# Gated DeltaNet layer on one core: GpSimd's order, two divided convolutions, and GpSimd's tile operations in quarters

## The reference

```python
h = rms_norm(x, norm_w) * (1 + scale) + shift            # scale, shift, gate from silu(c) @ ada_w + ada_b
q, k, v, z, b, a = split(h @ w_in)                       # 6160 columns
q, k, v = silu(causal_short_conv(concat(q, k, v), conv_w))   # 4 taps
q, k = l2_norm(q) * DK**-0.5, l2_norm(k)
beta, g = sigmoid(b), -exp(a_log) * softplus(a + dt_bias)
# S_t = exp(g_t)(I - beta_t k_t k_t^T) S_{t-1} + beta_t k_t v_t^T ; o_t = S_t^T q_t, chunk by chunk
o = gated_delta_rule_chunked(q, k, v, beta, g)
o = rms_norm(o, gdn_norm_w) * silu(z)
x = x + gate * (o @ w_out)
out = rms_norm(x, final_norm_w)
```

## Time and profile before

| | us |
|---|---|
| median of 3 runs | 1336.01 (1328.7 to 1340.26) |
| the profiled execution | 1332.38 |
| its span, first to last instruction | 1330.6 |
| PE busy | 1140.6 (86%) |
| DVE busy | 875.3 (66%) |
| POOL busy | 510.6 (38%) |
| mean granted TensorE clock | 0.945 of full speed |

### The profile page before, as it was taken

How to read it: one execution, slowest core, us unless ns; L and a number is a source line. 1 busy time by engine, 2 the same in 40 slices (tenths; PEclk the granted TensorE clock), 3 DMA queues, 4 the chain that set the end, 5 groups by cost and what they waited for, 6 DMA issues and landing times.

```text
span 1330.6 us, 18988 instructions
## 1 busy us (share of the span) xinstructions
PE 1140.6 (86%) x5572; PEld 926.7 (70%) x5572; DVE 875.3 (66%) x1881; ACT 444.0 (33%) x1022; POOL 510.6 (38%) x433
## 2 busy tenths in 40 slices
PE   1385589998899899998899989998899889999885
PEld 1353567877687778877787768777787778777763
DVE  4574657576776758575775758575766757586845
ACT  2232142333333242333333243323333243324333
POOL 2021253336433353345433353345433363345413
PEclk9588798999999999999999999999999999999998
DMA  6523132211322132211222122212212131212202
GB/s 240 206 73 111 37 88 51 58 36 48 74 50 56 48 77 51 56 36 49 73 50 56 52 72 51 56 39 65 62 47 52 52 81 42 56 39 70 51 33 110
DMA packets 143494, 88.34 MB, mean 66 GB/s; under 512 B 29350, under 2 KB 137032, under 8 KB 142408
## 3 DMA queue, kind: packets, MB, share of 16 engines
q1 hardware_dynamic: 143432, 87.73, 23.8%
HBM read 78.28 MB, written 9.44 MB: 66 GB/s over the span
## 4 chain that ended last, share of the span: by engine, by line
PE 52%; issue 19%; DVE 12%; POOL 8%; DMA 5%; ACT 3%; DVEq 0%; SPq 0%; POOLq 0%; ACTq 0%
PE bank L381 22%; PE bank L479 15%; DVE work L857 4%; POOL w_lo L1232 4%; POOL wo_lo L1238 2%; DMA w_raw<-in_gdn_w_in 2%; PE bank L522 2%; PE bank L439 2%; DVE y L890 2%; DMA work<-in_ada_w 2%; PE bank L532 1%; PE bank L535 1%; ACT w_hi L626 1%; PE bank L510 1%; PE bank L514 1%
## 5 line engine op out<-in xcount | busy, mean ns | idle before, releaser
L1232 POOL TENSOR_TENSOR w_lo<-w_raw,w_hi 128x1024 fp32r<-128x1024 f32 x96 | 244.7, 2549 | 425.3 <-ACT w_hi L626 425.3
L381 PE MATMUL bank<-h_hi,w_hi 128*128 128x512 f32 x768 | 323.7, 421 | 8.9 <-POOL w_lo L1232 4.5
L381 PE MATMUL bank<-h_hi,w_lo 128*128 128x512 f32 x768 | 319.1, 415 | 0.0
L381 PE MATMUL bank<-h_lo,w_hi 128*128 128x512 f32 x768 | 316.1, 412 | 0.0
L857 DVE SCALAR_TENSOR_TENSOR work<-pre,cw,work 128x512 f32<-128x512 f32 x192 | 212.1, 1104 | 23.6 <-DVE work L854 6.5
L381 PEld LDWEIGHTS bank<-h_hi,w_hi 128*128 128x128 f32 x768 | 150.2, 196 | 41.5 <-POOL w_lo L1232 8.0
L381 PEld LDWEIGHTS bank<-h_hi,w_lo 128*128 128x128 f32 x768 | 149.1, 194 | 31.4
L381 PEld LDWEIGHTS bank<-h_lo,w_hi 128*128 128x128 f32 x768 | 148.0, 193 | 29.0
L479 PE MATMUL bank<-wo_hi,og_hi 128*128 128x512 f32 x256 | 118.7, 464 | 53.4 <-POOL og_lo L1278 25.2
L652 ACT ACTIVATE work<-work 128x512 f32<-128x512 f32 x64 | 40.3, 629 | 302.3 <-DVE pre L865 176.8
L1278 POOL TENSOR_TENSOR og_lo<-work,og_hi 128x256 fp32r<-128x256 f32 x64 | 53.6, 837 | 208.8 <-ACT og_hi L686 208.8
(11 more groups left out here) (167 smaller groups left out, 1802.1 us busy)
## 6 DMA issues: line engine op xcount, KB each, us to landing
w_raw<-in_gdn_w_in SPq DMA_DIRECT2D x96, 512.0 KB, 4.0
work<-in_ada_w SPq DMA_DIRECT2D x8, 1024.0 KB, 5.0
w_raw<-in_gdn_w_out SPq DMA_DIRECT2D x16, 512.0 KB, 3.4
y<-in_x SPq DMA_DIRECT2D x2, 2048.0 KB, 9.1
work<-in_ada_w SPq DMA_DIRECT2D x8, 512.0 KB, 4.0
n_dram<-work SPq DMA_DIRECT2D x16, 256.0 KB, 3.4
out<-y SPq DMA_DIRECT2D x8, 512.0 KB, 2.6
t_dram<-work SPq DMA_DIRECT2D x16, 64.0 KB, 1.6
```

The source lines that it names most:

```text
L381: mm = nc.tensor.matmul(bank[m % 2][:, :], w[:, m % 2, k, :], h[:, k, half, :], start=(r == 0), stop=(r == MM - 1))
L1232: nc.gpsimd.tensor_tensor(w_lo[:, k % 2, :, :], w_raw_k[:, k % 2, :, :], w_hi[:, k % 2, :, :].bitcast(F32), ALU.subtract).then_inc(S["w_lo ...
```

## The change

Four edits:

- POOL in the recurrence of every unit but the last: tile 4 of `w_lo` stays in step 0; in step 1 the low half of the gated output now comes ahead of tile 5 of `w_lo`.
- DVE: the convolution `conv(u - 1, other, hd, 3)` at the head of the merge stage is divided: taps 0 and 1, then `merge_d_out(u, 0)`, then taps 2 and 3. The SiLU behind it (L874) moves behind `merge_p_out(u, 1)`. The convolution of q is divided too: taps 0 and 1 stay in step 1, taps 2 and 3 stand in step 2 behind `gate_o`.
- ACT, step 2: `og_high` now stands ahead of the tanh that waits for that convolution.
- POOL: `split_lo`, `split_wo` and `gate_wo` are four instructions on 128x256 each in place of one on 128x1024; only the last of the four raises the semaphore.

```diff
@@ ACT, recurrence
                     scale_x(u, par, c)
+                    if c > 0:
+                        og_high(u, c - 1)
                     if not last and c == 2:
                         tanh(u, 3, 1, cvq[:, other, :])
-                    if c > 0:
-                        og_high(u, c - 1)
@@ DVE, merge stage
                 silu(u - 1, 4, cvv[:, 0, :])
-                conv(u - 1, other, hd, 3)
+                conv(u - 1, other, hd, 3, range(0, 2))
                 merge_d_out(u, 0)
+                conv(u - 1, other, hd, 3, range(2, 4))
+                merge_p_out(u, 1)
                 silu(u - 1, 5, cvv[:, 1, :])
-                merge_p_out(u, 1)
                 if not last:
                     conv(u, par, nxt, 0)
@@ DVE, recurrence
                     if c > 0:
                         gate_o(u, c - 1)
+                    if not last and c == 2:
+                        conv(u, par, nxt, 1, range(2, 4))
                     passed(dve, "kv_done", u, c + 1)
...
                         elif c == 1:
-                            conv(u, par, nxt, 1)
+                            conv(u, par, nxt, 1, range(0, 2))
@@ POOL
             def split_lo(u, k):
                 passed(pool, "w_hi_done", u, k + 1)
                 passed(pool, "projected", u, k - 1)
-                nc.gpsimd.tensor_tensor(w_lo[:, k % 2, :, :], w_raw_k[:, k % 2, :, :],
-                                        w_hi[:, k % 2, :, :].bitcast(F32), ALU.subtract
-                                        ).then_inc(S["w_lo_done"], 1)
+                for j in range(0, KT, 2):
+                    i = nc.gpsimd.tensor_tensor(w_lo[:, k % 2, j:j + 2, :], w_raw_k[:, k % 2, j:j + 2, :],
+                                                w_hi[:, k % 2, j:j + 2, :].bitcast(F32), ALU.subtract)
+                i.then_inc(S["w_lo_done"], 1)
...
                 for c in range(NCH):
-                    if not last:
-                        if c < 2:
-                            split_lo(u, 4 + c)
+                    if not last and c == 0:
+                        split_lo(u, 4)
                     if c > 0:
                         og_low(u, c - 1)
-                    if not last and c == 2:
+                    if not last and c == 1:
+                        split_lo(u, 5)
+                    elif not last and c == 2:
                         split_lo(u + 1, 0)
                     power_o(u, c)
```

More of the change, by code:

```diff
@@ L1231, in split_lo @@
                 passed(pool, "projected", u, k - 1)
-                nc.gpsimd.tensor_tensor(w_lo[:, k % 2, :, :], w_raw_k[:, k % 2, :, :],
-                                        w_hi[:, k % 2, :, :].bitcast(F32), ALU.subtract
-                                        ).then_inc(S["w_lo_done"], 1)
+                for j in range(0, KT, 2):
+                    i = nc.gpsimd.tensor_tensor(w_lo[:, k % 2, j:j + 2, :], w_raw_k[:, k % 2, j:j + 2, :],
+                                                w_hi[:, k % 2, j:j + 2, :].bitcast(F32), ALU.subtract)
+                i.then_inc(S["w_lo_done"], 1)
             def split_wo(hd, i):
                 wo_passed(pool, "wo_hi_done", hd, i + 1)
-                nc.gpsimd.tensor_tensor(wo_lo[:, i, :], w_raw[:, 1 - i, :], wo_hi[:, i, :].bitcast(F32), ALU.subtract
-                                        ).then_inc(S["wo_lo_done"], 1)
+                for j in range(0, D_MODEL, 256):
+                    o = nc.gpsimd.tensor_tensor(wo_lo[:, i, j:j + 256], w_raw[:, 1 - i, j:j + 256],
+                                                wo_hi[:, i, j:j + 256].bitcast(F32), ALU.subtract)
+                o.then_inc(S["wo_lo_done"], 1)
             def gate_wo(hd, i):
                 tile_landed(pool, hd, 0, f"wo{i}")
-                nc.gpsimd.tensor_tensor(w_raw[:, 1 - i, :], w_raw[:, 1 - i, :], gate_bc[:, :], ALU.mult
-                                        ).then_inc(S["wo_gated"], 1)
+                for j in range(0, D_MODEL, 256):
+                    o = nc.gpsimd.tensor_tensor(w_raw[:, 1 - i, j:j + 256], w_raw[:, 1 - i, j:j + 256],
+                                                gate_bc[:, j:j + 256], ALU.mult)
+                o.then_inc(S["wo_gated"], 1)
             def mask_g(u):
```

## The result

| | before | after |
|---|---|---|
| median of 4 runs, us | 1333.95 (1328.7 to 1340.26) | 1286.57 (1284.31 to 1288.04) |
| the profiled execution, us | 1332.38 | 1286.46 |
| its span, us | 1330.6 | 1284.7 |
| mean granted TensorE clock | 0.945 | 0.959 |

The ratio is 0.965 (0.9622 to 0.9678): 3.5% faster. 1314 was forecast, a gain of 1.65%. The time lies inside the range, near its lower end, where the rival "PE keeps most of what it gains" stood with 1286.

A forecast was written before the change was run, and what follows sets the result against it. PE, busy 86% of the span, was taken as the bound, with DVE setting the unit's end after the change. 15 x -2.0 = -30 and 8 x 1.0 = +8 gave -22 us, forecast 1314 us, range 1282 to 1340.

The forecast's parts named there:

- PE keeps most of what it gains: Rival: quarters slip into DVE's PSUM operations; 3.6 us won in each of 15 units, less 4, so 1286; chance 0.20.
- PE's stall at L479 goes, and the slow clock with it: Step 2: with `og_lo` ahead of the weight tile, PE's 3.01 us wait ends; PE alone would allow 4.8 us a unit.
- I take -2.0 us for a unit: Net gain of each of 15 units, with DVE setting the unit's end: 15 x 2.0 = -30 us.
- Both waits come from PE being late, and go: -3.6: DVE, from the convolution to the odd unit's end: idle times of 3.02 and 0.56 us vanish.
- the sign that DVE alone does not set the end: Sign of being wrong: DVE with idle time left in steps 2 and 3, meaning PE sets the end after all.
- 5.3 remain: +1.4: POOL's hold on DVE beside its two-operand work: 5.3 us after against 3.9 before, costing a unit 1.4 us.
- A new wait at L510 of 0.9 us, 1.5 with POOL's `og_lo`: Step 3: PE waits for the state, delayed by two taps behind `gate_o`; 1.5 us if `og_lo` runs between the taps.
- A quarter 0.70, the tile 2.8: POOL's tile operations: 0.70 us for a quarter, 2.8 for a tile, 0.4 more than the 2.412 of the whole operation.
- L439's wait shrinks, PE waits about 3 us at L390, and again a slow clock: Even merge stage: 3.91 us shrinks to about 0.3; PE then waits for k's SiLU, with 1.7 us of slow clock.
- Tile 4: +1.0 us for an even unit: Even units' weight-tile chain: tile 4 ends at 639.6, not 636.00, costing 8 x 1.0 = +8 us.
- slower: queued quarters don't let DVE in: Rival: POOL's next quarter takes the ports before a waiting tap, so DVE waits 2.96 us; +16, 1352; chance 0.13.
- comes out even: Rival: full-cost quarters, L510 wait nearer 2 us, weight chain losing 2; 15 x 1.2 = -18 against +16, 1334; chance 0.25.

The follow-up runs named there:

- e1: The kernel before with the new order of POOL and ACT alone, whole convolutions and whole tile operations; 1335.05 us, ratio 1.0012.
- e9: The kernel before with the new order of POOL and ACT and the quarters, both convolutions whole; 1287.84 us, ratio 0.9668.
- e12: The changed kernel with quarters for tiles 0 and 5, halves elsewhere, and q's convolution divided three taps to one; 1277.07 us, ratio 0.958.
- e6: The changed kernel with the convolution of q whole again in step 1; 1291.93 us, ratio 0.968.

## Why the prediction was right in sign and short in size

The difference of the two spans, -45.9 us against -22 predicted, cut at the starts of L410 of units 1 to 15 in each trace. The predicted column shares out the -2.0 of each unit and the +1.0 of each even one:

| us | predicted | measured |
|---|---|---|
| to the L410 of unit 1 (prologue and unit 0) | -1.0 | -5.7 |
| 7 odd units | -14.0 | -23.6 |
| 6 even units in the loop | -6.0 | -16.2 |
| the even unit behind the loop | -1.0 | +1.3 |
| the end | 0 | -1.5 |

**"PE's stall at L479 goes, and the slow clock with it"**: right, in full. The 9.61 us of the earlier trace rows became 4.75. That `r` must be earlier for it was in the prediction ("a whole convolution stood before it"), and e1 shows it: without that the order is worth nothing. But the division wasn't needed for most of it: with the quarters alone beside the order (e9), `r` is still 1.8 us late and the gain is nearly whole.

**"I take -2.0 us for a unit"**: the term that was mis-sized most. Steps 2 and 3 gave 2.8 us in the odd unit and 2.9 in the even one, and 15 x 0.8 = 12 us of the missing 24 are here. Both halves of its working were off, in opposite directions. "Both waits come from PE being late, and go: -3.6": DVE kept 1.6 us of waiting for PE (0.80 and 0.57 above, and 0.20 before the next gated output), so only 2.0 went. I had named this as the sign that DVE alone does not set the end, and so it is: the two engines wait for each other in turn. "5.3 remain: +1.4" is where the mechanism failed, since POOL holds DVE up for 3.5 us, not 5.3: 0.4 in L854 and 0.25 in a tap, beside the two `og_lo`; 0.3 in the tap of 1.04; 0.15, 0.46 and 0.46 in the small operations beside the first tile, and 1.5 in the four beside the second. That is -0.4 against the 3.9 before. -2.0 and -0.4 make -2.4 of the measured -2.8; the last 0.4 is in short gaps between DVE's instructions, 1.7 us before and 1.4 after. So it is luck that the sum of -2.2 came near -2.4: 1.8 us too much for POOL stood against 1.6 too much won from the waits.

I had each quarter hold DVE for its whole 0.70 us, and a waiting small operation is held for 0.46. The Trainium skill, page SBUF — State Buffer, section "SBUF: two separate sides", says that the lock is held for a whole instruction; in these rows it looks free for a part of what the profile shows as one. So it was nearly the mechanism of the rival "PE keeps most", "DVE is held up no more than today", though not its 3.6 for a unit. That its 1286 is the measured time is luck in part: it had 54 us from the 15 units, less 4 for the chain of tiles. Steps 2 and 3 gave 42, and 4 more came from the odd units' merge stages and step 1, which it left at nothing.

**"A new wait at L510 of 0.9 us, 1.5 with POOL's `og_lo`"**: right at 0.94, although `og_lo` did come between. It ends step 2 and is counted there. The wait for `y` behind it, 0.61 us, was not in my list: in step 3 L479 starts 1.75 us behind L510 and not 0.77, and that is the whole +0.95 of step 3. It did not go when e12 took the wait at L510 away, where step 3 still takes 13.2.

**"A quarter 0.70, the tile 2.8"**: right, 2.82 beside nothing. The 2.6 cycles for an element of the Trainium skill, page GPSIMD Engine Reference, section "Elementwise — side-by-side cycle accounting", give an estimate of 2.2 for the tile, and the rows are longer, whole (2.41) and in quarters.

**"L439's wait shrinks, PE waits about 3 us at L390, and again a slow clock"**: the wait came, at 2.1 to 2.4 us, with the slow clock in units 2 and 4 and without it in the other four of the loop. The merge stage ran 3.3 us shorter in unit 6. I had the SiLU 2.2 us earlier, and it ended 3.1 us earlier (22.5 us behind L410 and not 25.6). 0.8 of that lies ahead of the first tap: over the even units DVE was idle 1.3 to 2.2 us there before, 0.8 to 1.2 after. Its cause stays open.

**"Tile 4: +1.0 us for an even unit"**: wrong. Counted from L410, PE takes tile 4 at 45.35 us where it took it at 46.67, 1.3 earlier. But PE arrives 3.3 us earlier, waits 2.72 us in place of 0.77, and has the slow clock behind it, so that step 2 starts no earlier than before: +3.3 in step 1 against -3.3 ahead of it, so 0 for the even unit and not +1.0. That is 8 x 1.0 = 8 of the missing 24. With the 12 above and 7 x 0.6 = 4 from the merge stage and step 1 of the odd units, where I had 0, it is about the whole; the other lines of the table (unit 0, whose step 2 alone gave 5.1, the last even unit and the end) differ from mine by -4.7, +2.3 and -1.5, of which unit 0 and the last even unit are partly in those terms.

**The rival "slower: queued quarters don't let DVE in"**: ruled out. The rows show one small operation of DVE for each quarter, in turn, and the longest tap is 1.411 us, not 2.9:

```profile
L857 DVE SCALAR_TENSOR_TENSOR work<-pre,cw,work x192: 740/753/1411, 73.3 to 1228.5; 128x512 f32<-128x512 f32 x192
```

**The rival "comes out even"** had its price right in one place: the chain of the even unit has no slack, and takes back what the merge stage wins. Its -1.2 us for a unit was not: steps 2 and 3 gave 2.8, and the clock behind the wait at L510 stayed at 1.00.

## What to carry to other kernels

When a stall goes, look at what stands ahead of the *second* thing that its engine will wait for. Here an order alone gave nothing and two more edits, each a loss by itself, made it worth 3.5% (one of them, the quarters, 3.3%); so edits that clear one path are to be judged together, and taken away one at a time. A long instruction that holds another engine up is worth cutting, but not finely: whole tiles and eighths each lost about half of the gain here, halves and quarters kept it, and each cut had a price of its own (0.12 to 0.14 us) in the chain that waits for the last piece. And a gain ahead of a chain with no slack comes back as a wait, which is priced with the clock behind it.

## What the runs showed of the hardware

- Small two-operand DVE instructions of 0.2 us beside quarters on POOL follow each other every 0.69 us, which is the time of POOL's own quarters undisturbed (2.82/4 = 0.70): they delay POOL by nothing that can be seen, and each is itself held for 0.46 us.
- Stalls of one length do not always have the same sequel. In e6, after 1.80 us of waiting PE's granted clock stayed at 1.00 in one unit and was 0.77 over the stretch behind it in another. In the kernel after, 2.15 us before L390 had 0.66 behind it in unit 4, and 2.16 us had 1.00 in unit 6. In the kernel before, 3.16 us before L479 had 1.00 over the next 4 us in units 2 and 8, and 0.59 to 0.65 in units 4, 6, 10 and 12.
